# Rounding the weights of the dense chunks one level ahead between the levels of a packed triangular inverse

## The reference

```python
def _gated_delta_chunked(q, k, v, beta, g):          # chunk c = 64, 4 heads, 2 directions
    decay = exp(where(incl, gc[..., :, None] - gc[..., None, :], -inf))
    lmat = where(strict, einsum('bhnid,bhnjd->bhnij', kb, k) * decay, 0.0)
    tmat = lmat + eye(c)
    sol = triangular_solve(tmat, concatenate([v * beta, kb * exp(gc)]), lower=True, unit_diagonal=True)
    ...
def layer(x):
    h = _rmsnorm(x, attn_norm_w[l])
    (g_qkv, g_z, ..., gate_raw) = _split_cols(h @ w_in[l])      # dense projections of h
    ...
    x = x + merged @ w_out[l]
    x = x + _hier_moe(_rmsnorm(x, ffn_norm_w[l]), ...)           # 32 experts, SwiGLU
```

## Time and profile before

| | us |
|---|---|
| median of 3 runs | 1672.69 |
| lowest and highest of them | 1667.34, 1673.09 |
| profiled execution, its own time | 1666.46 |
| its span in the trace | 1664.6 |
| TensorE busy in the span | 1324.1 (80%) |
| VectorE, ScalarE, GpSimd busy | 669.3, 465.4, 117.6 |
| mean granted TensorE clock | 0.938 of full |

### The profile page before, as it was taken

One profiled execution on the slowest core, in us unless ns is written; L12 is line 12 of the kernel. 1 busy time (PEld: TensorE's weight loads), 2 busy tenths in 40 slices (PEclk: granted clock), 3 DMA queues, 4 the chain that ended last, 5 costly groups with the idle time before them and its releaser, 6 DMA issues. The chain is left out here.

```text
span 1664.6 us, 46417 instructions
## 1 busy us (share of the span) xinstructions
PE 1324.1 (80%) x19424; PEld 1018.4 (61%) x19425; DVE 669.3 (40%) x1620; ACT 465.4 (28%) x948; POOL 117.6 (7%) x106
## 2 busy tenths in 40 slices
PE   6997789998967676667889987999879766667665
PEld 5786677775645454445577775877656544445453
DVE  6657746654211111111276657575532211111112
ACT  3446436442100000000045454454421100000001
POOL 2002440000000000000010034300000000000000
PEclk9999899999999999998999988999999999998998
DMA  9531006487999999999974210245879999999996
GB/s 305 209 132 51 1 8 225 173 334 256 428 428 428 428 428 428 428 428 428 417 270 153 101 51 2 93 161 202 353 316 407 428 428 428 428 428 428 428 428 279
DMA packets 76723, 490.22 MB, mean 294 GB/s; under 512 B 12878, under 2 KB 15462, under 8 KB 52070
## 3 DMA queue, kind: packets, MB, share of 16 engines
q1 hardware_dynamic: 76646, 489.16, 72.2%
HBM read 488.09 MB, written 1.05 MB: 294 GB/s over the span
## 5 line engine op out<-in xcount | busy, mean ns | idle before, releaser
L1905 PE MATMUL ps<-ring,arena 128*32 128x128 f32 x5760 | 208.4, 307 | 153.4 <-DMA ring<-in_expert_w_up_dram 93.8
L1905 PEld LDWEIGHTS ps<-ring,arena 128*32 128x32 f32 x5760 | 181.3, 124 | 175.4 <-DMA ring<-in_expert_w_up_dram 102.7
L2068 DVE COPY arena<-ps 128x256 f32<-128x256 f32 x68 | 28.9, 424 | 327.0 <-PE ps L1878 326.9
L1980 ACT ACTIVATE arena<-ps 128x128 f32<-128x128 f32 x66 | 18.3, 277 | 481.1 <-PE ps L1905 481.1
L1905 PE MATMUL ps<-arena 128*32 128x128 f32 x2688 | 90.5, 293 | 66.5 <-DMA arena<-in_expert_w_up_dram 41.2
L1905 PEld LDWEIGHTS ps<-arena 128*32 128x32 f32 x2688 | 78.6, 118 | 76.6 <-DMA arena<-in_expert_w_up_dram 45.2
L460 POOL TENSOR_TENSOR small<-small,cst 128x8 f32<-128x8 f32 (+1 forms) x21 | 27.4, 1305 | 1253.4 <-DVE small L705 461.8
L1694 DVE TENSOR_TENSOR w_low<-ring,w_high 128x512 fp32r<-128x512 f32 x128 | 87.0, 705 | 52.9 <-ACT w_high L1625 52.9
L1625 ACT ACTIVATE w_high<-ring 128x512 fp32r<-128x512 f32 x128 | 78.7, 634 | 88.7 <-PE ps L1562 71.8
L1923 PE MATMUL ps<-ring,arena 128*32 128x256 f32 x1440 | 87.6, 382 | 5.2 <-DMA ring<-in_expert_w_down_dram 2.7
L1878 PE MATMUL ps<-xn,arena 128*32 128x256 f32 x1088 | 83.6, 430 | 7.5 <-DVE arena L2063 7.3
(11 more groups left out here) (351 smaller groups left out, 2452.7 us busy)
## 6 DMA issues: line engine op xcount, KB each, us to landing
ring<-in_expert_w_gate_dram SPq DMA_DIRECT2D x44, 2048.0 KB, 41.8
ring<-in_expert_w_up_dram SPq DMA_DIRECT2D x44, 2048.0 KB, 40.6
ring<-in_expert_w_down_dram SPq DMA_DIRECT2D x44, 2048.0 KB, 40.6
ring<-in_w_in_dram SPq DMA_DIRECT2D x28, 2048.0 KB, 8.5
arena<-in_expert_w_gate_dram SPq DMA_DIRECT2D x20, 2048.0 KB, 41.8
arena<-in_expert_w_up_dram SPq DMA_DIRECT2D x20, 2048.0 KB, 41.1
arena<-in_expert_w_down_dram SPq DMA_DIRECT2D x20, 2048.0 KB, 40.9
ring<-in_w_out_dram SPq DMA_DIRECT2D x4, 2048.0 KB, 7.8
```

Of the source, the lines that this page charges most:

```text
L1905: ins = pe.matmul(bank_b[32 * g:32 * g + 32, u * P:(u + 1) * P], xg[:, c], w[:, u, c, g], start=(c == 0), stop=(c == KC - 1))
L2068: v.tensor_copy(rows, bank_a[:, 0:256]).then_inc(m_rows, 1)
```

## The change

ScalarE rounds chunk 4 ahead of the first level, and in levels 1 to 3 it rounds the chunk of the next level (5, 6, 7) where it had rounded that of the same level. Level 4 rounds nothing. Nothing is added, and nothing is taken away; GpSimd's, VectorE's and TensorE's programs stay as they are.

```diff
@@ -1325,6 +1325,7 @@
                     act.wait_ge(e_t, 2 * (n - 1) + d + 1)
                     act.activation(XTB[:, 2 * d:2 * d + 2], t_at[d][:, 0:2 * P].rearrange("p (g b i) -> p g b i", g=2, b=4), ACT.Copy).then_inc(e_xt, 1)
 
+                early_high(4)
                 act.wait_ge(e_zero, 2)
                 for n in range(1, LEVELS):
                     for d in range(2):
@@ -1334,7 +1335,8 @@
                     d, p = divmod(n - 1, 2)
                     b1, b2 = first_second(d, p)
                     act.activation(LTO[quarter(b1), half_of(d)], LTm[quarter(b1), half_of(d), quarter(b2)], ACT.Copy).then_inc(e_lto, 1)
-                    early_high(3 + n)
+                    if n < LEVELS - 1:
+                        early_high(4 + n)
```

## The result

| | before | changed |
|---|---|---|
| median | 1672.89 us (4 runs) | 1650.74 us (4 runs) |
| lowest to highest | 1667.34 to 1674.17 | 1650.25 to 1653.45 |
| ratio, 95% interval | | 0.9882 [0.9855, 0.9910] |
| profiled execution, its span | 1666.46, 1664.6 | 1650.25, 1648.4 |

The change makes the kernel faster, by 22 us on these medians and by 16.2 us between the two profiled executions. The difference between the two figures is the spread of the runs of before. 16.2 us of 1672.7 is 0.9903, which lies in both intervals.

A forecast was written before the change was run, and what follows sets the result against it. The expert stages were taken as bound by weights, the changed block as held by TensorE's waits, then by VectorE. Levels gain 17.8 us, less 1.6 ahead of level 1: 16.2, so 1672.69 becomes 1656.5 us, range 1646 to 1665.

The forecast's parts named there:

- The waits go: In the levels of both layers, all eight TensorE waits for low parts, about 2 us each, disappear.
- It is passed on: Behind the block, everything starts earlier by what it saves, some 7 us in layer 1 and 9 more in layer 2.
- VectorE binds at 4.8, 4.8, 4.8, 4.6 us: Levels 1 to 4 of each layer are bound by VectorE's work at these times, 19.0 us a layer.
- the 5.3 us: In the levels, any level over 5.3 us was to show the prediction wrong.
- the 4.7 to 4.9 us between masks: In the levels, VectorE's mask L1461 starting every 4.7 to 4.9 us was to show the prediction right.
- 0.8 us ahead of level 1: Ahead of level 1, GpSimd's subtraction of chunk 4 holds VectorE's L1446, costing 0.8 us a layer, bounds 0 and 1.27.
- the 23 clears: Behind GpSimd's memset ahead of level 1, 23 clears at 44 ns delay the subtraction of chunk 4 by 1.0 us.
- the clock stays low: Rival: half clock through all levels leaves a gain of 4.6 us, 1668.1 us; chance 0.10.
- eight waits of 2 us are 15.8 us: Check of the sum from TensorE's waits in both layers: 15.8 us, beside the forecast gain of 16.2 us.
- The size: Whole kernel: 16.2 us gained, profiled execution from 1666.46 to 1650.3 us, median from 1672.69 to 1656.5 us.
- VectorE is not held: Rival: subtractions slip off the levels' spreads, TensorE binds at 4.1 us a level; 23.0 us gained, 1649.7 us; chance 0.08.
- The slower rival: Rival: later product blocks meet 19 more half-clock stretches, kernel over 0.5% slower, 1682 us; chance 0.02.

The follow-up runs named there:

- e3: Kernel before the change, each level's own chunk rounded between ScalarE's spreads and turned copies, without look-ahead: 1646.63 us, 0.9881 of the kernel before.
- f1: Kernel before the change, with 12 unused TensorE matmuls ahead of each dense product in the levels, filling its waits: 1663.26 us, 0.9959 of the kernel before.
- f2: Changed kernel with 18 unused TensorE matmuls ahead of level 1: 1649.55 us, 0.9873 of the kernel before.
- e4: Changed kernel, look-ahead kept, with the roundings of levels 1 to 3 put between spreads and turned copies: 1651.57 us, 0.9906 of the kernel before.
- g2: Changed kernel run again unaltered, in another set of runs: 1652.31 us, 0.9910 of the kernel before.
- f3: Kernel before the change with only chunk 4 rounded ahead of level 1, chunks 5 to 7 in levels 2 to 4 as before: 1671.54 us, 1.0010.
- e2: Kernel before the change, with each level's rounding put ahead of the LTO copy: 1668.98 us, 1.0009 of the kernel before.

## Why the prediction was right

- *The waits go.* Right: no wait of TensorE for a low part is left, and e3 and f1 show from two sides that they were paid.
- *It is passed on.* Right: 17.5 us from the two blocks, and 1339 us of other stages that change by 1.0. The blocks are 7.7 and 9.9 us shorter, for 7 and 9 forecast.
- *VectorE binds at 4.8, 4.8, 4.8, 4.6 us.* The mechanism was right, the sizes were off both ways. Level 1 took 5.72 and 5.20, since the clock fell in it; f2 brings it to 4.70. The 5.72 is over the 5.3 us that the prediction named as a sign of being wrong, and its dense product took 2.0 us (194.84 to 196.84), not 1.5. Level 2 took 4.63 and 4.67. Level 3 took 4.29, and level 4 took 4.02, the term that was most over-sized (4.6): its copies, L1485 before, took 1.36 us for 2.02 once the subtraction of chunk 7 had gone. So only level 2 comes near the 4.7 to 4.9 us between masks that were to show it right. The sum was forecast at 19.0 and measured at 18.66 and 18.19. e3 and e4 show the hold-up of the spreads to be 0.2 to 0.6 us a level, less than the 1.0 us by which a copy is drawn out, because TensorE's own 4.07 us lie right under it.
- *0.8 us ahead of level 1.* Measured 0.90 and 0.66, and 1.3 to 1.7 in the repeat (g2) and in two kernels with the same rounding of chunk 4 (e4, f3); that is past the bound of 1.27 that the prediction had set. The cause named was right: a VectorE instruction with two operands in SBUF is held by that subtraction, though it is a different one from trace to trace. Within it one step failed: the 23 clears were taken as 1.0 us of delay. In layer 1 the subtraction followed the memset at once, and what it held was not L1446 but a copy ahead of it:

```profile
183.15 1.29 POOL L1379 TENSOR_TENSOR w_low<-ring,early_w_high 128x512 fp32r<-128x512 f32 x1
...
183.74 3.87 DVE L1433 COPY arena<-arena 32x256 f32<-32x256 f32 x2
...
184.38 1.81 POOL L1390 MEMSET arena<- 128x2048 f32 x1
...
186.15 1.31 POOL L1379 TENSOR_TENSOR w_low<-ring,early_w_high 128x512 fp32r<-128x512 f32 x1
```

  Two copies that take 0.28 us each at best stood until 187.61 beside three GpSimd instructions in a row. The first took 2.59 us, across the end of `early_low(3)` and the whole memset, and the second 1.28 us, with the subtraction of chunk 4. In layer 2 it was L1448 of the second direction (L1446 before), as forecast: 1.03 us for 0.38.
- *The clock.* The sum had it only inside the levels' old times. It deserved a term of its own: 7.1 of the 19.0 us. The rival "the clock stays low" came true in level 1 alone. TensorE's idle time ahead of it, taken as 2.7 us, was 4.20 and 2.20, and 3.00 in layer 1 of g2.
- *The check "eight waits of 2 us are 15.8 us"* agreed by chance. By f1 it is 7.1 us from the clock and the other 11.8 from the waits, less 1.6 ahead of level 1. f3 shows how the waits alone mislead: two of the eight removed, 4 us by such a count, gave 3.2 us in the levels and 0.2 in the blocks, and the times show nothing.
- *The size.* 16.2 us were forecast from the profiled execution and 16.2 were measured between the profiled ones. The blocks gave 17.5; the agreement to the tenth has luck in it, as the first stretch alone differed by 2.4 us. The median was forecast at 1656.5 and measured at 1650.74, 5.8 us lower.
- *Two slips of arithmetic that change nothing.* The rival "VectorE is not held" leaves out the 1.6 us ahead of level 1: by its own terms it is 21.4 us and 1651.3, not 23.0 and 1649.7. The slower rival's 1682 should be 1681.

What stays open: why f3 and e2 meet half clock in just those levels, and whether single runs without a trace meet it in the same ones.

## What to carry to other kernels

Before you move a piece of work earlier, ask which engine's idle slot it and its followers land in: the rounding in ScalarE's gap between spreads and turned copies did better than a whole level of look-ahead. The larger part of that is that no subtraction is left ahead of level 1 (e3 against e4, 5.1 us over the two blocks); that the subtractions in the levels met VectorE instructions that they don't hold gave 0.7 to 1.0 us a layer (e4). When TensorE waits for some 2 us again and again, read the granted clock of the work behind the wait and price both; filling the wait with unused matmuls separates them. A small step that shortens waits can show nothing in the time and still be right.

## What was not expected of the hardware

- 96 unused matmuls made the kernel 7 us faster (0.9959 [0.9943, 0.9975]): with TensorE at work in its 2 us waits the granted clock stayed at 1.00 over 28 us, where it had been 0.88.
- A GpSimd memset of 1.81 us held VectorE copies as a subtraction does, and a copy can be held across two GpSimd instructions in a row (one took 2.59 us for 0.28). The 23 semaphore clears behind the memset took no visible time: it ended at 186.19, and the next GpSimd instruction started at 186.15.
